# The mean of a layer norm is subtracted on VectorE, up to three tiles ahead of the multiplication, instead of on GpSimd

## The chip, the core and the metric

The kernel runs on one core of a Trainium2 chip. TensorE multiplies matrices, VectorE and ScalarE work element by element, GpSimd is a slower general engine that also issues some of the DMAs, and SyncE issues the weight loads. In the profile they are PE, DVE, ACT, POOL and SP. The metric is the device time of one execution in microseconds (us).

## The reference

One step of a two-layer decoder for 528 prompt tokens (16 of them learned meta tokens) and 32 tokens of eight running sequences, 560 columns in all, with a model width of 1024. What matters here is the layer norm. There are five of them: one on the embedded input, and two in each layer, one behind the token mixer and one behind the convolutional feed-forward block (the FFN).

```python
def layer_norm(x, g, b):
    xf = x.astype(jnp.float32)
    mu = jnp.mean(xf, -1, keepdims=True)
    var = jnp.mean(jnp.square(xf - mu), -1, keepdims=True)
    return ((xf - mu) * lax.rsqrt(var + LN_EPS) * g + b).astype(x.dtype)
...
x = layer_norm(embedded, emb_ln_g, emb_ln_b)
for l in range(DEPTH):
    mix, ... = token_mixer(x, ...)        # x @ w_in, HGRN2 heads, retention heads, @ w_o
    x = layer_norm(ALPHA * x + mix, ln1_g[l], ln1_b[l])
    ffn, ... = conv_ffn(x, ...)           # x @ w_a, x @ w_b, convolution, gelu, @ w_down
    x = layer_norm(ALPHA * x + ffn, ln2_g[l], ln2_b[l])
```

## The kernel before

Activations are stored with features on the partitions: `X` holds 8 tiles (`KT`) of 128 features by 560 columns in fp32. For the matmuls every tile is split into two fp16 parts, `XH` and the remainder `XL`, and the weights likewise into `WH` (made by ScalarE, `split_hi`, L825) and `WL` (made by VectorE, `split_lo`, L1149). TensorE forms three products for each pair of parts.

The order of the work is written out by hand. Each engine has its own program, a queue in strict order, and the engines meet through semaphores: `wait_ge(sem, n)` stops a queue until the counter is n. In the layer loop n is computed from a register, in the last norm it is a constant. `dve.drain()` makes the next VectorE instruction wait until the ones before it have written their results; it stands wherever one VectorE instruction reads what a near predecessor on the same engine wrote.

A norm, `norm_apply` on three engines and `norm_stats` on TensorE, goes like this:

- TensorE forms the mean of x (L486; for the first norm L477) and the mean of x squared (L491) over the 1024 features as matmuls with a matrix of 1/1024.
- ScalarE copies the mean to `MU` (L837) and squares it into `MSQ` (L838). VectorE subtracts `MSQ` from the mean square (L1180, two halves) and clips the variance at 0 (L1184, the "max" below). ScalarE takes its logarithm (L841) and the exponential of minus half of that (L843): `RSTD` is ready.
- GpSimd, in `norm_centre`, subtracts `MU` from the 8 tiles of `X` in place (L404). It waits for the copy of the mean alone.
- VectorE runs a loop over m: it waits for GpSimd's subtraction of tile m and multiplies the tile by `RSTD` (L1189). From m = 2 on it then waits until ScalarE is through with tile m-2 and forms `XL` of that tile (L1192).
- ScalarE applies gain and bias twice for each tile, to `XH` in fp16 (L848) and to `X` in fp32 (L849). In the last norm there is no `XH` and no `XL`.

Behind a norm, TensorE starts a `gemm_pair`: two output tiles at once, 12 matmuls for each k of the 8 tiles, in the order in which `XL` comes (`x_ready`). The matmuls are at L506. ScalarE, when it is done with the norm's tiles, goes on with the next `split_hi` (L825; behind the second norm of a layer comes first the load of the gelu table, L1079), VectorE follows with `split_lo` (L1149), and TensorE needs that `WL` for its third output tile. In a mixer VectorE's next step is `hg_gate` (L1198), behind that same `split_lo`. Behind the last norm TensorE transposes `X` (L797) once all eight tiles are done, and the result is copied and stored.

GpSimd's queue holds, in order: in each layer the first `norm_centre`, the load of the convolution state, the heads' states (a load, two products, two stores for each head, `head_states`, DMA issues at L398), the second `norm_centre`, the stores of the convolution state; and at the end the `norm_centre` of the last norm.

Of the kernel before, what the change touches and what calls it, by code (L numbers as in the profile page):

```python
# [25 lines left out]
ALU = mybir.AluOpType  # L26
ACT = mybir.ActivationFunctionType
# [3 lines left out]
DEPTH = 2  # L31
# [14 lines left out]
T = TP + TS  # L46
HALF = T // 2
KT = D_MODEL // P
# [28 lines left out]
O_TILE, F_TILE, D_TILE = 32, 40, 40 + 2 * FT  # L77

SCR_START = (11, 6, 5)
SCR_LN = (2, 1, 1)  # L80
# [90 lines left out]
def hybrid_decoder_step(nc, x_prompt, x_sample, state_hgrn, state_ret, state_conv, meta_tokens, emb_ln_g, emb_ln_b,  # L171
# [23 lines left out]
    with ExitStack() as ctx:  # L195
# [3 lines left out]
        def sem(name):  # L199
            return ctx.enter_context(nc.semaphore(name))  # L200

        tab = sb("tab", [P, n_const])
        X = sb("X", [P, KT, T])
# [29 lines left out]
        S1, S2, SQT, MU, MSQ, VAR, RSTD = B, Q, E, T1, T2, T3, QS  # L233
# [46 lines left out]
        y_ready, sq_ready, sq_used, sums_ready = sem("y_ready"), sem("sq_ready"), sem("sq_used"), sem("sums_ready")  # L280
        mu_ready, msq_ready, var_ready, rstd_ready = sem("mu_ready"), sem("msq_ready"), sem("var_ready"), sem("rstd_ready")
        ln_mul, ln_sub, ln_out, x_ready = sem("ln_mul"), sem("ln_sub"), sem("ln_out"), sem("x_ready")
        f_ready, lnf_parts, f2_ready, k_ready = sem("f_ready"), sem("lnf_parts"), sem("f2_ready"), sem("k_ready")
# [16 lines left out]
        def halves(ap):  # L300
            return ap.rearrange("p (a n) -> p a n", a=2)
# [86 lines left out]
        def _(pool):  # L388
# [10 lines left out]

            def norm_centre(n):  # L400

                pool.wait_ge(mu_ready, n + 1)
                for m in range(KT):
                    nc.gpsimd.tensor_tensor(X[:, m, :], X[:, m, :], MU[:, 0:T], ALU.subtract).then_inc(ln_sub, 1)  # L404

            def head_states(l, p, kind, s0_v, sn_v, fin_v, fin_src):
# [16 lines left out]
            with pool.Fori(0, DEPTH) as l:  # L423
                norm_centre(2 * l)

                move((acc_full, 1 + l * TILES), CIN, cin_v[ds(l * 2 * DEC_BATCH, 2 * DEC_BATCH), :], cin_in)
                with pool.Fori(0, HEADS) as p:
                    head_states(l, p, 0, s0_hg_v, sn_hg_v, fin_hg_v, SC[:, (NC - 1) * P:NC * P])
                with pool.Fori(0, HEADS) as p:
                    head_states(l, p, 1, s0_rt_v, sn_rt_v, fin_rt_v, RSB[:, :])  # L430
                norm_centre(2 * l + 1)
                move((cso_ready, l + 1), cp_v[ds(l * 2, 2), :], CSO[0:2, :], cso_stored)
                move((cso_ready, l + 1), cs_v[ds(l * 2 * DEC_BATCH, 2 * DEC_BATCH), :], CSO[2:18, :], cso_stored)
            norm_centre(2 * DEPTH)
            pool.wait_ge(fin_stored, 16 + 16 * DEPTH * 2 * HEADS)
# [366 lines left out]
        def _(act):  # L802
# [31 lines left out]
            def norm_apply(n, ot, last=False):  # L834
                act.wait_ge(ot_full, ot + 1)
                src = OT[:, :, 0:HALF]
                f(halves(MU[:, 0:T]), src, ACT.Copy).then_inc(mu_ready, 1)  # L837
                f(halves(MSQ[:, 0:T]), src, ACT.Square).then_inc(ot_read, 1)  # L838
# [305 lines left out]
        def _(dve):  # L1144
# [29 lines left out]
            def norm_apply(n, scr, last=False):  # L1174
# [8 lines left out]

                ts(VAR[:, 0:T], VAR[:, 0:T], 0.0, None, ALU.max).then_inc(var_ready, 1)  # L1184
                dve.wait_ge(rstd_ready, n + 1)
                for m in range(KT + 2):
                    if m < KT:
                        dve.wait_ge(ln_sub, n * KT + m + 1)
                        tt(X[:, m, :], X[:, m, :], RSTD[:, 0:T], ALU.mult).then_inc(ln_mul, 1)  # L1189
                    if m >= 2 and not last:  # L1190
                        dve.wait_ge(ln_out, n * KT + m - 1)
                        tt(XL[:, m - 2, :], X[:, m - 2, :], XH[:, m - 2, :], ALU.subtract).then_inc(x_ready, 1)  # L1192
# [452 lines left out]
```

## Time and profile before

| | |
|---|---|
| median of 3 runs | 1770.37 us (1768.78 to 1770.78) |
| span of the profiled execution, first to last instruction | 1765.4 us |
| the profiled execution's own time | given by its span alone; the median of the runs is 5.0 us more than that span |
| busy: TensorE | 1585.4 us, 90% of the span |
| busy: VectorE | 930.3 us, 53% |
| busy: ScalarE | 657.9 us, 37% |
| busy: GpSimd | 154.2 us, 9% |
| GpSimd's subtractions (L404) | 40 instructions, 65.2 us |
| VectorE's multiplications by `RSTD` (L1189) | 40 instructions, 727 to 1906 ns each |

A norm is a stretch of 15 to 25 us in which TensorE has nearly nothing to do. Five of them lie in the span; their first multiplications start at 40.97, 488.43, 898.59, 1338.08 and 1740.30 us. Below they are called norms 0 to 4. Norms 0 and 2 stand ahead of a token mixer, norms 1 and 3 ahead of an FFN, norm 4 ahead of the output.

In a row of the timeline the first number is the start in us, the second the duration of the piece in us. Then come engine, line, operation, what is written from what, the shapes and the count (xN). In brackets stands how long the engine had been idle before, and who ended that.

### The profile page before, as it was taken

The numbers are of one execution on the slowest core, as the hardware profiler recorded it, in microseconds if no ns is written. First come the engines' busy times: TensorE is split into PE (matmuls) and PEld (weight loads), VectorE is DVE, ScalarE is ACT, GpSimd is POOL, SyncE is SP. The second block draws the span as 40 slices with busy tenths as digits, with TensorE's granted clock in tenths as the row PEclk, the third lists the DMA queues.
The fourth block names the chain that finished last, engine by engine and source line by source line (L and its number), as shares of the span: only waits on it lengthen the run. The fifth ranks groups of instructions, "written<-read, shape, count | busy, mean of one in ns | idle before, by whom it ended". The sixth has DMA issues, their size and how long they took to land.

```text
span 1765.4 us, 31743 instructions
## 1 busy us (share of the span) xinstructions
PE 1585.4 (90%) x12187; PEld 1263.6 (72%) x12187; DVE 930.3 (53%) x1493; ACT 657.9 (37%) x936; POOL 154.2 (9%) x126
## 2 busy tenths in 40 slices
PE   4699999998879999999957999999896999999994
PEld 3577777776658888878745777777674888887883
DVE  5766744443575555533266767444366555553334
ACT  3635423232263433422154544233235443333223
POOL 3111110000020000000030111100002000000002
PEclk8789889998989999999978989999987999999997
DMA  5121231220312233223321222222121323322321
GB/s 185 51 62 51 73 109 62 84 73 26 96 50 94 95 95 95 73 79 90 97 66 48 73 73 73 76 85 73 50 74 47 96 95 95 95 80 71 98 65 51
DMA packets 175036, 137.86 MB, mean 78 GB/s; under 512 B 5064, under 2 KB 169192, under 8 KB 174776
## 3 DMA queue, kind: packets, MB, share of 16 engines
q1 hardware_dynamic: 168192, 113.46, 21.1%
q0 software_dynamic: 5408, 18.60, 3.1%
q10 hardware_dynamic: 1372, 4.95, 0.8%
q8 instruction: 41, 0.67, 0.2%
q14 instruction: 23, 0.19, 0.0%
HBM read 124.91 MB, written 12.07 MB: 78 GB/s over the span
## 4 chain that ended last, share of the span: by engine, by line
PE 76%; DVE 10%; ACT 6%; issue 4%; DVEq 3%; ACTq 1%; DMA 1%; SPq 0%
PE ACC L506 60%; PE SCR L619 2%; PE SCR L536 2%; PE OT L627 2%; ACT WH L825 1%; PE SCR L657 1%; DVE X L1189 1%; PE OT L679 1%; DVE Z L1220 1%; PE OT L595 1%; DVE Fb L1202 1%; DVE WL L1149 1%; DVEq L1259 1%; PE SCR L722 1%; PE OT L594 1%
## 5 line engine op out<-in xcount | busy, mean ns | idle before, releaser
L506 PE MATMUL ACC<-XH,WH 128*128 128x280 f16 x2432 | 503.7, 290 | 74.7 <-DVE XL L1192 43.1
L506 PE MATMUL ACC<-XL,WH 128*128 128x280 f16 x2432 | 502.6, 289 | 0.0
L506 PE MATMUL ACC<-XH,WL 128*128 128x280 f16 x2432 | 502.2, 289 | 0.0
L506 PEld LDWEIGHTS ACC<-XH,WH 128*128 128x128 f16 x2432 | 237.4, 101 | 158.7 <-DVE XL L1192 45.9
L1149 DVE SCALAR_TENSOR_TENSOR WL<-stage,WH 128x2048 f16<-128x2048 f32 (+1 forms) x116 | 245.9, 2120 | 180.8 <-ACT WH L825 169.1
L506 PEld LDWEIGHTS ACC<-XL,WH 128*128 128x128 f16 x2432 | 243.4, 100 | 58.8
L506 PEld LDWEIGHTS ACC<-XH,WL 128*128 128x128 f16 x2432 | 243.5, 100 | 58.4
L825 ACT ACTIVATE WH<-stage 128x2048 f16<-128x2048 f32 (+1 forms) x116 | 204.8, 1765 | 103.0 <-PE ACC L506 85.7
L506 PE MATMUL ACC<-shared,WH 128*128 128x280 f16 x1408 | 225.4, 283 | 0.2
L506 PEld LDWEIGHTS ACC<-shared,WH 128*128 128x128 f16 x1408 | 137.6, 98 | 30.7 <-issue 0.8
L506 PE MATMUL ACC<-shared,WL 128*128 128x280 f16 x704 | 141.3, 283 | 0.0
L404 POOL TENSOR_TENSOR X<-X,T 128x560 f32<-128x560 f32 x40 | 65.2, 1664 | 424.7 <-ACT T L837 424.7
L832 ACT ACTIVATE E<-X 128x560 f32 (+1 forms) x32 | 21.5, 671 | 192.9 <-DVEq L1171 192.9
L506 PE MATMUL ACC<-OHL,WH 128*128 128x280 f16 x512 | 87.8, 297 | 6.0 <-DVE X L1169 6.0
L1169 DVE SCALAR_TENSOR_TENSOR X<-ACC,X 128x560 f32 (+1 forms) x32 | 23.7, 740 | 109.7 <-PE ACC L506 109.0
L506 PEld LDWEIGHTS ACC<-shared,WL 128*128 128x128 f16 x704 | 68.9, 98 | 15.1
L1089 ACT ACTIVATE T<-ACC 128x560 f32<-128x560 f32 x44 | 28.1, 639 | 135.5 <-PE ACC L506 135.2
L506 PEld LDWEIGHTS ACC<-OHL,WH 128*128 128x128 f16 x512 | 51.6, 103 | 22.6 <-DVE X L1169 7.0
L1568 DVE SCALAR_TENSOR_TENSOR Fb<-ACC,Fb 128x560 f32<-128x560 f32 x22 | 16.3, 742 | 92.3 <-PE ACC L506 92.3
L413 POOL TENSOR_TENSOR VX<-KVTS,tab 32x1024 f32<-32x1024 f32 x16 | 30.2, 1886 | 306.3 <-ACTq L916 218.7
L619 PE MATMUL SCR<-VX,KVTS 32*128 32x512 f32 x64 | 39.6, 724 | 19.2 <-DVE shared L1350 19.2
L1551 DVE COPY AS<-T 128x32 f32<-128x32 f32 x44 | 8.0, 182 | 90.0 <-ACTq L1092 89.6
(241 smaller groups left out, 1870.7 us busy)
## 6 DMA issues: line engine op xcount, KB each, us to landing
stage<-in_w_in_dram SPq DMA_DIRECT2D x64, 512.0 KB, 4.8
stage<-in_w_a_dram SPq DMA_DIRECT2D x44, 512.0 KB, 4.2
stage<-in_w_b_dram SPq DMA_DIRECT2D x44, 512.0 KB, 4.6
stage<-in_w_down_dram SPq DMA_DIRECT2D x32, 384.0 KB, 3.1
stage<-in_w_down_dram SPq DMA_DIRECT2D x32, 320.0 KB, 3.4
out_dram<-shared POOLq DMA_DIRECT2D x16, 512.0 KB, 3.4
stage<-in_w_o_dram SPq DMA_DIRECT2D x16, 512.0 KB, 3.9
shared<-in_state_hgrn_dram POOLq DMA_DIRECT2D x8, 512.0 KB, 5.8
```

Source lines behind the costliest of these rows:

```text
L404: nc.gpsimd.tensor_tensor(X[:, m, :], X[:, m, :], MU[:, 0:T], ALU.subtract).then_inc(ln_sub, 1)
L413: nc.gpsimd.tensor_tensor(VX[:, :, :], KVTS[:, 1:2, :].to_broadcast([TS, DEC_BATCH, P]), bcast(seqm[0:TS, :], P), ALU.mult).then_inc(vx_re ...
L506: last = mm(ACC[:, acc, h, 0:HALF], lhs, x[:, xk + k, h * HALF:(h + 1) * HALF], start=begin, stop=end)
L536: last = mm(SCR[0:w, bank, o:o + w], keys[:, t:t + w], queries[:, t:t + w], start=True, stop=True)
L594: mm(o, SC[:, (c - 1) * P:c * P], QD[:, t:t + w], start=True, stop=False)
L619: mm(SCR[:, bank, :], KVTS[:, 0, :], VX[:, 4 * n:4 * n + 4, :].rearrange("p b v -> p (b v)"), start=True, stop=True).then_inc(scr_full, 1)
L627: last = mm(OT[:, 1, TP - SPLIT + DEC_SEQ * b:TP - SPLIT + DEC_SEQ * (b + 1)], S0b[:, b, :], qs[:, TP + DEC_SEQ * b:TP + DEC_SEQ * (b + 1) ...
L825: f(WH[:, s, 0:width], stage[:, s, 0:width], ACT.Copy, scale=W_SCALE).then_inc(w_hi[s], 1)
L832: f(SQT[:, 0:T], src, ACT.Square).then_inc(sq_ready, 1)
L1089: f(halves(AX[c][:, 2:2 + T]), ACC[:, c, :, 0:HALF], ACT.Copy, scale=INV_W)
L1149: stt(out=WL[:, s, 0:width], in0=stage[:, s, 0:width], scalar=W_SCALE, in1=WH[:, s, 0:width], op0=ALU.mult, op1=ALU.subtract).then_inc(w_l ...
L1169: stt(out=halves(row(m)), in0=ACC[:, c, :, 0:HALF], scalar=INV_W / ALPHA, in1=halves(row(m)), op0=ALU.mult, op1=ALU.add).then_inc(acc_read ...
```

## The change

GpSimd's `norm_centre` goes, with its three calls and the two semaphores `mu_ready` and `ln_sub`. VectorE does the same 40 subtractions of [128 x 560] in place. Three of them (`AHEAD`) stand between the max and the wait for `RSTD`, with one drain behind them. In the loop the subtraction of tile m+3 stands right behind the multiplication of tile m, for m = 0 to 4, each followed by a drain. Nothing else is changed; GpSimd's other work stays in its order.

```diff
+AHEAD = 3
...
-            def norm_centre(n):
-
-                pool.wait_ge(mu_ready, n + 1)
-                for m in range(KT):
-                    nc.gpsimd.tensor_tensor(X[:, m, :], X[:, m, :], MU[:, 0:T], ALU.subtract).then_inc(ln_sub, 1)
-
...
             with pool.Fori(0, DEPTH) as l:
-                norm_centre(2 * l)
-
                 move((acc_full, 1 + l * TILES), CIN, cin_v[ds(l * 2 * DEC_BATCH, 2 * DEC_BATCH), :], cin_in)
...
-                norm_centre(2 * l + 1)
                 move((cso_ready, l + 1), cp_v[ds(l * 2, 2), :], CSO[0:2, :], cso_stored)
...
-            norm_centre(2 * DEPTH)
...
             def norm_apply(n, ot, last=False):
                 act.wait_ge(ot_full, ot + 1)
                 src = OT[:, :, 0:HALF]
-                f(halves(MU[:, 0:T]), src, ACT.Copy).then_inc(mu_ready, 1)
+                f(halves(MU[:, 0:T]), src, ACT.Copy)
...
                 ts(VAR[:, 0:T], VAR[:, 0:T], 0.0, None, ALU.max).then_inc(var_ready, 1)
+                for m in range(AHEAD):
+                    tt(X[:, m, :], X[:, m, :], MU[:, 0:T], ALU.subtract)
+                dve.drain()
                 dve.wait_ge(rstd_ready, n + 1)
                 for m in range(KT + 2):
                     if m < KT:
-                        dve.wait_ge(ln_sub, n * KT + m + 1)
                         tt(X[:, m, :], X[:, m, :], RSTD[:, 0:T], ALU.mult).then_inc(ln_mul, 1)
+                    if m + AHEAD < KT:
+                        tt(X[:, m + AHEAD, :], X[:, m + AHEAD, :], MU[:, 0:T], ALU.subtract)
+                        dve.drain()
                     if m >= 2 and not last:
                         dve.wait_ge(ln_out, n * KT + m - 1)
                         tt(XL[:, m - 2, :], X[:, m - 2, :], XH[:, m - 2, :], ALU.subtract).then_inc(x_ready, 1)
```

## Rows read from the trace of the kernel before

**Rows 1.** The page: its head, and the chain that ended last, by engine.

```profile
span 1765.4 us, 31743 instructions
...
PE 76%; DVE 10%; ACT 6%; issue 4%; DVEq 3%; ACTq 1%; DMA 1%; SPq 0%
```

**Rows 2.** Windows, max to first multiplication: length, PE, PEld, DVE, ACT, POOL, clock, DMA.

```profile
37.93:40.97 3.04, 0.00 (x0) 0.00 (x0) 1.27 (x2) 1.43 (x2) 3.04 (x3) 0.50 0.83 251
485.15:488.43 3.28, 0.00 (x0) 0.00 (x0) 1.49 (x2) 1.43 (x2) 3.28 (x3) 0.72 0.00 0
895.52:898.59 3.07, 0.00 (x0) 0.00 (x0) 1.29 (x1) 1.43 (x2) 3.07 (x3) 0.50 0.15 45
1334.99:1338.08 3.09, 0.00 (x0) 0.00 (x0) 1.30 (x2) 1.43 (x2) 3.09 (x3) 0.50 0.00 0
1737.15:1740.30 3.15, 0.00 (x0) 0.00 (x0) 1.58 (x2) 1.43 (x2) 3.15 (x3) 0.83 0.00 0
```

**Rows 3.** Timeline of norm 1: GpSimd, and VectorE where GpSimd ends.

```profile
483.65 12.82 POOL L404 TENSOR_TENSOR X<-X,T 128x560 f32<-128x560 f32 x8 [64.27 <-ACT T L837]
...
495.17 1.91 DVE L1189 TENSOR_TENSOR X<-X,QS 128x560 f32<-128x560 f32 x1
497.00 0.73 DVE L1192 TENSOR_TENSOR XL<-X,XH 128x560 f16<-128x560 f32 x1
497.65 0.73 DVE L1189 TENSOR_TENSOR X<-X,QS 128x560 f32<-128x560 f32 x1
```

**Rows 4.** Window from the first multiplication to TensorE's first matmul, L1189 alone.

```profile
488.43:495.31 6.88, 5.13 (x4) 0.50 0.00 0
```

**Rows 5.** ScalarE's timeline: tile 3 of norm 1; first instruction behind norms 0 to 2.

```profile
56.09 1.89 ACT L825 ACTIVATE WH<-stage 128x2048 f16<-128x2048 f32 x1
...
497.24 0.85 ACT L848 ACTIVATE XH<-X,par 128x560 f16<-128x560 f32 x1 [2.05 <-DVE X L1189]
...
504.82 1.28 ACT L1079 ACT_TABLE_LOAD   x1
...
914.89 1.90 ACT L825 ACTIVATE WH<-stage 128x2048 f16<-128x2048 f32 x1
```

**Rows 6.** Timelines: what continues behind norms 0, 1 and 2, and its releaser.

```profile
61.33 0.74 DVE L1198 TENSOR_SCALAR Fb<-ACC 128x560 f32<-128x560 f32 x1 [1.02 <-PE ACC L506]
...
510.48 0.41 PE L506 MATMUL ACC<-XH,WH 128*128 128x280 f16 x2 [1.18 <-DVE WL L1149]
...
919.02 0.73 DVE L1198 TENSOR_SCALAR Fb<-ACC 128x560 f32<-128x560 f32 x1
```

**Rows 7.** Timeline of norm 4: all eight multiplications, and TensorE's next matmul.

```profile
1740.30 10.82 DVE L1189 TENSOR_TENSOR X<-X,QS 128x560 f32<-128x560 f32 x8 [1.57 <-ACT QS L843]
...
1752.34 5.31 PE L797 MATMUL SCR<-tab,X 128*128 128x128 f32 x24 [16.42 <-ACT X L849]
```

**Rows 8.** VectorE's timeline: a drain between two instructions; a drain and a wait.

```profile
512.89 0.18 DVE L1551 COPY AS<-T 128x32 f32<-128x32 f32 x1 [0.20 <-issue]
...
922.60 0.73 DVE L1203 TENSOR_TENSOR T<-T 128x560 f32<-128x560 f32 x1
923.41 0.45 DVE L1205 TENSOR_SCALAR T<-T 128x560 f32<-128x560 f32 x1
```

**Rows 9.** TensorE's windows in norm 1's pair: busy us (matmuls), clock, DMA.

```profile
495.31:500.30 4.99, 4.99 (x22) 0.51 0.00 0
...
500.30:509.30 9.00, 9.00 (x76) 1.00 0.00 0
```

**Rows 10.** Timelines in norm 0: a DMA that GpSimd issues, VectorE beside it.

```profile
47.69 0.93 POOL L398 DMA_DIRECT2D shared<-in_state_hgrn_dram  x1
...
47.73 0.73 DVE L1189 TENSOR_TENSOR X<-X,QS 128x560 f32<-128x560 f32 x1
```

**Rows 11.** TensorE's timeline: the matmuls of the mean, norms 1 and 3.

```profile
481.69 1.21 PE L486 MATMUL OT<-B,tab 128*128 128x280 f32 x4 [3.03 <-DVEq L1175]
...
1330.31 2.23 PE L486 MATMUL OT<-B,tab 128*128 128x280 f32 x4 [3.02 <-DVEq L1175]
```

More of the change, by code:

```diff
@@ L280, in hybrid_decoder_step @@
         y_ready, sq_ready, sq_used, sums_ready = sem("y_ready"), sem("sq_ready"), sem("sq_used"), sem("sums_ready")
-        mu_ready, msq_ready, var_ready, rstd_ready = sem("mu_ready"), sem("msq_ready"), sem("var_ready"), sem("rstd_ready")
-        ln_mul, ln_sub, ln_out, x_ready = sem("ln_mul"), sem("ln_sub"), sem("ln_out"), sem("x_ready")
+        msq_ready, var_ready, rstd_ready = sem("msq_ready"), sem("var_ready"), sem("rstd_ready")
+        ln_mul, ln_out, x_ready = sem("ln_mul"), sem("ln_out"), sem("x_ready")
         f_ready, lnf_parts, f2_ready, k_ready = sem("f_ready"), sem("lnf_parts"), sem("f2_ready"), sem("k_ready")
```

## The prediction

> **What bounds the kernel now.** I read the page first. The chain that ended last is 76% TensorE and 10% VectorE [rows 1]; GpSimd does not appear in it. So the subtractions that the change takes from GpSimd are on no path by themselves. The next view was the timeline around the five norms, engine by engine, because there TensorE waits for the other engines.
>
> In norm 1 GpSimd is busy from 483.65 to 496.47 us, 1.60 us for a tile, and VectorE's first multiplication starts at 488.43, when about three tiles are done. GpSimd stays ahead, so the multiplications do not wait for it. They run slowly instead: the one at 495.17 takes 1.91 us and its successor starts 1.83 us later; from 497.00, half a microsecond after GpSimd's end, an instruction of the same size takes 0.73 us and the next starts 0.65 us later [rows 3]. The max shows the same: 1.27 to 1.58 us in the five norms, in which GpSimd is busy throughout [rows 2], against 0.45 us for the same operation on the same shape where GpSimd is idle [rows 8]. What GpSimd costs here is the speed of VectorE beside it.
>
> The third reading is what VectorE's delay holds up. TensorE starts its pair on the first `XL`, 6.88 us behind the first multiplication (four such stretches, 6.88 to 6.89) [rows 4]. Behind the pair the releasers differ: norm 0 goes on at the end of the pair, norm 1 at `WL`, norm 2 right behind `WL` with no idle time [rows 6]. `WL` follows ScalarE's last tile, whose successor on ScalarE starts 15.12, 16.39 and 16.30 us behind the first multiplication in norms 0, 1 and 2 [rows 5], and in norm 3 as in norm 1. In norm 4 everything waits for ScalarE's last tile, 12.04 us behind the first multiplication [rows 7].
>
> **The change part by part.** *The stretch from the max to the first multiplication.* It takes 3.04, 3.28, 3.07, 3.09 and 3.15 us in norms 0 to 4 [rows 2]. After the change the max should take 0.45 us, as without GpSimd [rows 8]. An instruction of 0.73 us lets an independent successor start 0.08 before its end [rows 3]; so the first subtraction starts at 0.37 and the third ends 0.65 + 0.65 + 0.73 = 2.03 later, at 2.40. `RSTD` needs 1.77 us behind the max (3.04 - 1.27) and would be there at 2.22, so the subtractions now end last, by 0.2 to 0.4 us. A drain costs 0.08 us from end to start between two plain instructions, and 0.20 where a wait on a computed count follows [rows 8]. I take 0.20 in norms 0 to 3, where the count comes from a register, and 0.08 in norm 4, where it is constant: 2.60 and 2.48 us. Gains: 0.44, 0.68, 0.47, 0.49 and 0.67.
>
> *The loop, norms 0 to 3*, from the start of the first multiplication. A multiplication with its subtraction and a drain takes 0.65 + 0.73 + 0.08 = 1.46. Three of these rounds reach 4.38; the third drain has a wait behind it, so the first `XL` starts at 4.50 and ends at 5.23. TensorE starts 0.05 later, at 5.28 against 6.88: a gain of 1.60. Multiplication 3 starts at 5.15; rounds 3 and 4 take 0.65 + 0.73 + 0.20 + 0.65 = 2.23 each, so multiplication 5 starts at 9.61; rounds 5 and 6 take 1.30 each, and multiplication 7 runs from 12.21 to 12.94. ScalarE starts a tile 0.16 behind its multiplication (495.17 + 1.91 to 497.24 [rows 3, 5]) and takes 1.50 for it (five tiles from 497.24 to 504.82 [rows 5]). Its next instruction can start at 14.60: gains 0.52, 1.79, 1.70 and 1.79 in norms 0 to 3.
>
> *What follows.* Norm 0 continues at the pair's end: 0.44 + 1.60 = 2.04. Norms 1 to 3 hang on ScalarE's end: 0.68 + 1.79 = 2.47, 0.47 + 1.70 = 2.17, 0.49 + 1.79 = 2.28. Their pairs end 2.28, 2.07 and 2.09 earlier, and TensorE had 1.18 us of idle time in norm 1 [rows 6], so the pair does not take over.
>
> *Does the later supply starve TensorE?* A tile of the pair is 12 matmuls: 12 x 4.99 / 22 = 2.7 us at the 1.2 GHz level, with which each pair begins, and 12 x 9.00 / 76 = 1.4 at 2.4 GHz [rows 9]. `XL` comes every 2.23 us at first and then every 1.30. Tile 1 is wanted at 5.28 + 2.7 = 8.0 and there at 7.5, tile 2 is wanted near 10.4 and there at 9.7, tile 3 near 11.8 against 11.0. It holds, with half a microsecond to spare.
>
> *Norm 4.* No `XL`: five rounds of 1.46, then 0.65 each; multiplication 7 runs from 8.60 to 9.33. ScalarE does three tiles from 8.19 (0.16 behind multiplication 5), 0.75 apart (half a tile's 1.50), and ends its last, of 0.85, at 10.54; TensorE starts at 10.59 against 12.04: 1.45, with the front 2.12.
>
> *GpSimd's queue.* The subtractions stood ahead of a state load, which is issued in 0.93 us [rows 10]. It moves to the front of the norm in norms 0 and 2. The chain has 1% of DMA [rows 1], so I count an earlier arrival as nothing. At worst the issue holds VectorE for its 0.93 us in both, 1.9 in all; the multiplication at 47.73 took 0.73 beside such an issue [rows 10], so I take nothing. ScalarE's copy loses only a signal.
>
> *Sum:* 2.04 + 2.47 + 2.17 + 2.28 + 2.12 = 11.1 us. The profiled span is 1765.4 us and the median 5.0 above it; a saving inside the span passes to both: 1754.3 and **1759.2**.
>
> *Bounds.* If every drain costs 0.08, norm 0 gains 0.24 and norms 1 to 3 gain 0.48 each more: 12.8. If every drain costs 0.20, the pair starts 0.24 later, ScalarE's end comes 0.24 later, and norm 4 loses 0.7: 9.4. TensorE's clock moves it further: the four matmuls of the mean take 1.21 us in norm 1 and 2.23 in norm 3, after 3.03 and 3.02 us of idle time [rows 11], so the level there is a matter of phase. From their start to the max it is 3.46 and 4.68 us [rows 2, 11], a swing of 1.2. Norms 1 and 4 could fall to the lower level, norm 3 could rise. That makes 7.0 to 14.0.
>
> **A rule against it.** The rows say that a VectorE instruction starts 0.08 us before its independent predecessor has ended [rows 3]. The Trainium skill, "VectorE: DVE Perf Modes", section "The DRAIN you can't avoid", says that the next instruction does not start until the pipe has emptied. The trace does not agree: 0.65 us from start to start for 0.73 us of length [rows 3]. By the rule the new instructions would cost their whole length and the gain would be 6.3 us (rival 1), by the rows it is 11.1.
>
> **The rivals.**
>
> 1. *No overlap between VectorE's instructions.* Each step without a drain costs 0.73 instead of 0.65. Up to the first `XL` that is six steps (0.48 us, norm 0), up to ScalarE's end fifteen (1.20, norms 1 to 3), in norm 4 ten (0.80): 4.9 us less, 1764.1. Against it stands the spacing in [rows 3]. Chance 0.05.
> 2. *The clock does not move with the pair.* If TensorE's rise to 2.4 GHz stays at its old instant, the time gained ahead of it is run at half speed. The pairs then gain half (1.0, 1.1, 1.0, 1.0) and become what ends last; with norm 4's 2.1 the gain is 6.3 and the time 1764.1. For it: the low stretch lasts 4.99 us in norm 1, and nothing in a row ties its end to the start. Against: all four pairs begin low, wherever they lie. Chance 0.07.
> 3. *The mixers give it back.* Behind norms 0 and 2 come the mixers, where three engines hand work to each other; if a weight load or a state sets the pace there, only norms 1, 3 and 4 count: 6.9 us, 1763.5. Against it: the chain shows 1% DMA [rows 1]. Chance 0.05.
> 4. *Slower: VectorE's slowness is not GpSimd's doing* but comes from working on `X` beside ScalarE. Then the subtractions cost 1.83 a step as the multiplications do. In norm 1 ten steps and 1.1 us lead to TensorE's start, against 3.28 + 6.88 now, so it turns at 0.90 us a step; at 1.83 and a max of 1.49 it costs 10 us a norm, in norm 4 sixteen: 56 in all, 1826. For it: slow and fast instructions both occur in one norm. Against: from 497.00 VectorE is fast while ScalarE still has five tiles to do [rows 3, 5]. Chance 0.03.
> 5. *Two of the first three at once*: 1.5 us or so are left, 1769. Chance 0.05.
>
> The forecast has 0.75.
>
> **How the numbers follow.** 0.2% (3.5 us) is about what a measurement of this kernel can tell from no change. Forecast and rivals 1 to 3 are faster by more: 0.92. Rival 5 is within it: 0.05. Rival 4 is slower: 0.03. The bounds of the sum give 1756.4 to 1763.4; the range takes in rivals 1 to 3 at 1764 and a microsecond below, 1755.5 to 1764.5.
>
> **What would show it.** In the profile after: the max near 0.45 us and the first multiplication 2.5 to 2.6 behind the max's start; multiplications, subtractions and `XL` all at 0.73; TensorE's first matmul about 5.3 behind the first multiplication and never waiting for a later `XL`; ScalarE's next instruction at 14.6; stretches behind the norms unchanged in length. Multiplications near 1.8 would overthrow the reading of GpSimd; waits of TensorE inside a pair, or pairs that grow as their start moves forward, would cut the gain to about half.

## The result, and the profile after

Median 1751.57 us (1749.42 to 1752.87, 4 runs) against 1770.19 us (1768.78 to 1770.78, 4 runs) before: ratio 0.9899 [0.9883, 0.9915], 18.6 us faster. I had forecast 11.1 and a range of 1755.5 to 1764.5, so the time lies 4 us outside it on the fast side. A second measurement (e5 below) gave 0.9923 [0.9902, 0.9943], 13.9 us, inside the range. Two executions far outside all others (2114 us of e2, 6357 us of the kernel before, timed beside e1 to e4) are left out everywhere.

The page of the changed kernel, head and chain, against [rows 1]:

```profile
span 1749.8 us, 31782 instructions
...
PE 74%; DVE 10%; ACT 6%; DVEq 4%; issue 3%; ACTq 1%; DMA 1%; SPq 0%
```

The spans differ by 15.6 us. The rest of the 18.6 is that the profiled execution of before was one of its faster ones: its span was 4.8 us below the median of the four, where the changed kernel's own time, 1751.54, is 1.7 above its span.

**The norms.** Windows of the changed kernel from the max to the first multiplication, norms 0 to 4, columns as in [rows 2]:

```profile
38.45:40.93 2.48, 0.00 (x0) 0.00 (x0) 2.41 (x4) 1.43 (x2) 0.00 (x0) 0.50 1.00 302
476.11:478.59 2.48, 0.00 (x0) 0.00 (x0) 2.41 (x4) 1.43 (x2) 0.00 (x0) 0.50 0.00 0
885.68:888.17 2.49, 0.00 (x0) 0.00 (x0) 2.40 (x4) 1.43 (x2) 0.00 (x0) 0.50 0.88 274
1322.83:1325.31 2.48, 0.00 (x0) 0.00 (x0) 2.40 (x5) 1.43 (x2) 0.00 (x0) 0.50 0.00 0
1723.95:1726.43 2.48, 0.00 (x0) 0.00 (x0) 2.40 (x4) 1.43 (x2) 0.00 (x0) 1.00 0.00 0
```

All five are 2.48 or 2.49 (forecast 2.60, and 2.48 in norm 4). VectorE's timeline in norm 1, against [rows 3]:

```profile
476.11 0.45 DVE L1175 TENSOR_SCALAR T<-T 128x560 f32<-128x560 f32 x1
476.48 2.04 DVE L1177 TENSOR_TENSOR X<-X,T 128x560 f32<-128x560 f32 x3
478.59 0.74 DVE L1182 TENSOR_TENSOR X<-X,QS 128x560 f32<-128x560 f32 x1
479.25 0.73 DVE L1184 TENSOR_TENSOR X<-X,T 128x560 f32<-128x560 f32 x1
480.06 0.74 DVE L1182 TENSOR_TENSOR X<-X,QS 128x560 f32<-128x560 f32 x1
...
483.09 0.74 DVE L1188 TENSOR_TENSOR XL<-X,XH 128x560 f16<-128x560 f32 x1 [0.17 <-issue]
```

The max is at 0.45 us, the three subtractions take 2.04 (forecast 2.03), a round takes 480.06 - 478.59 = 1.47 (1.46), the first `XL` starts 4.50 us behind the first multiplication (4.50). What used to take up to 1.91 us beside GpSimd takes 0.74. TensorE and ScalarE in the same norm, against [rows 4] and [rows 5]:

```profile
471.44 2.23 PE L477 MATMUL OT<-B,tab 128*128 128x280 f32 x4 [3.03 <-DVEq L1166]
...
483.89 0.65 PE L497 MATMUL ACC<-XH,WH 128*128 128x280 f16 x2 [8.36 <-DVE XL L1188]
...
487.98 0.40 PE L497 MATMUL ACC<-XH,WH 128*128 128x280 f16 x2
```

```profile
489.04 0.85 ACT L839 ACTIVATE XH<-X,par 128x560 f16<-128x560 f32 x1 [0.59 <-DVE X L1182]
...
493.65 1.28 ACT L1070 ACT_TABLE_LOAD   x1
```

TensorE starts 483.89 - 478.59 = 5.30 us behind the first multiplication (forecast 5.28, before 6.88), ScalarE's next instruction 15.06 behind it (14.60; before 16.39). The end of norm 4, against [rows 7]:

```profile
1733.77 2.04 DVE L1182 TENSOR_TENSOR X<-X,QS 128x560 f32<-128x560 f32 x3
...
1736.95 5.24 PE L788 MATMUL SCR<-tab,X 128*128 128x128 f32 x24 [13.59 <-ACT X L840]
```

From the first multiplication to TensorE it is 10.52 us (forecast 10.59, before 12.04). Counted from the start of the max to what continues, the norms went from 9.93 to 7.77 (norm 0, the pair's start), 19.67 to 17.54, 19.37 to 17.40, 19.49 to 17.53 (ScalarE's next instruction) and 15.19 to 13.00 (TensorE): 2.16 + 2.13 + 1.97 + 1.96 + 2.19 = 10.4 us. In norm 0 a part of this does not arrive. VectorE's timeline there, against the first of [rows 6]:

```profile
57.79 2.29 DVE L1140 SCALAR_TENSOR_TENSOR WL<-stage,WH 128x2048 f16<-128x2048 f32 x1 [1.06 <-ACT WH L816]
60.00 0.73 DVE L1194 TENSOR_SCALAR Fb<-ACC 128x560 f32<-128x560 f32 x1
```

Before, the read of `ACC` waited 1.02 us for the end of TensorE's pair. Now it stands right behind `WL` with no idle time: from the max it comes 60.00 - 38.45 = 21.55 us later, before 61.33 - 37.93 = 23.40, so norm 0 is worth 1.85 and not 2.16. That makes 10.1 us for the change's own work, 1.0 less than forecast. Repeated profiles agree: with norm 0 counted to ScalarE's first read of `Fb`, the five windows sum to 97.9 us before, and to 87.8 in the change and in e4, e5, e14 and e15 below, which leave the norms as they are in the change.

**The mixers.** TensorE's windows over the two mixers, before and then after: length, busy time (matmuls), granted clock, DMA. The first window runs from ScalarE's first read of `Fb` behind norm 0 to its copy of the mean in norm 1, the second from the fourth `Z` instruction of the first head (L884, L875 after) to the copy of the mean in norm 3.

```profile
62.10:482.90 420.80, 383.57 (x2737) 0.89 0.22 70
930.90:1332.60 401.70, 361.58 (x2646) 0.92 0.23 71
```

```profile
60.80:473.70 412.90, 372.78 (x2737) 0.93 0.23 72
919.10:1320.40 401.30, 361.15 (x2646) 0.93 0.23 71
```

The change touches nothing in these windows. Yet the first is 7.9 us shorter: the same 2737 matmuls take 10.8 us less at a granted clock of 0.93 in place of 0.89. Of the 15.6 us between the spans, 8.3 lie in the mixers and 7.3 in the rest. The rest keeps 7.3 of its own 10.1: 1.3 are lost at the start of layer 2 (below), 0.5 ahead of the first max (37.93 to 38.45; kernels that still subtract on GpSimd in norm 0 reach 38.9 there), and 1.0 in the second FFN and between the copies of the mean and the max. The trace of before could have warned me: 383.57 / 2737 = 140 ns a matmul in its first mixer and 361.58 / 2646 = 137 in its second, the same code at 0.89 and 0.92.

**The start of layer 2.** ScalarE's timeline there, before and then after:

```profile
882.27 0.67 ACT L832 ACTIVATE E<-X 128x560 f32<-128x560 f32 x1 [13.79 <-DVEq L1171]
885.12 1.28 ACT L1050 ACT_TABLE_LOAD   x1 [2.18 <-issue]
```

```profile
871.10 0.67 ACT L823 ACTIVATE E<-X 128x560 f32<-128x560 f32 x1 [13.79 <-DVEq L1162]
875.29 1.28 ACT L1041 ACT_TABLE_LOAD   x1 [3.52 <-issue]
```

GpSimd's timeline of the changed kernel at that instant:

```profile
870.88 0.49 POOL L399 DMA_DIRECT2D shared<-in_state_conv_dram  x1 [124.34 <-PE ACC L497]
```

The table load comes 4.19 instead of 2.85 us behind the square: a loss of 1.34 that I had not counted. The convolution state, whose load before was issued behind norm 2's subtractions, is now loaded just there. The DMA queues between the square and the table load, before and then after:

```profile
q14 instruction: 2, 0.02, 1.4%
```

```profile
q0 software_dynamic: 32, 0.18, 16.0%
q14 instruction: 2, 0.02, 1.6%
```

Before, the first of the two 8 KB packets of the instruction queue (q14) starts 1.28 us behind the square and takes 0.31. After, the load's packets (q0) run from 0.97 to 2.07 us behind the square, and that first packet starts at 1.96 and takes 0.75.

### The profile page after: what moved, and what is told of

The parts are those of the page before. It is cut to its first block, busy times and chain, and to the rows that moved or that the text cites. A ratio compares the mean times of both kernels' runs of the same rounds, so it can differ in the third digit from the quotient of the medians.

```text
span 1749.8 us, 31782 instructions
## 1 busy us (share of the span) xinstructions
PE 1575.6 (90%) x12187; PEld 1257.8 (72%) x12187; DVE 928.3 (53%) x1533; ACT 658.4 (38%) x936; POOL 89.3 (5%) x86
## 4 chain that ended last, share of the span: by engine, by line
PE 74%; DVE 10%; ACT 6%; DVEq 4%; issue 3%; ACTq 1%; DMA 1%; SPq 0%
PE ACC L497 58%; PE SCR L527 2%; PE SCR L610 2%; PE OT L618 2%; ACT WH L816 2%; PE SCR L648 1%; PE OT L670 1%; DVEq L1255 1%; DVE Z L1216 1%; DVE X L1182 1%; DVEq L1185 1%; DVE WL L1140 1%; PE OT L586 1%; DVE Fb L1198 1%; PE SCR L713 1%
## 5 line engine op out<-in xcount | busy, mean ns | idle before, releaser
L816 ACT ACTIVATE WH<-stage 128x2048 f16<-128x2048 f32 (+1 forms) x116 | 204.9, 1766 | 103.0 <-PE ACC L497 85.7
L497 PE MATMUL ACC<-OHL,WL 128*128 128x280 f16 x256 | 54.9, 298 | 0.0
L1090 ACT ACTIVATE shared<-Fb 128x560 f32 x22 | 14.8, 671 | 94.2 <-DVEq L1566 94.2
```

The costliest lines, as they stand in the source:

```text
L497: last = mm(ACC[:, acc, h, 0:HALF], lhs, x[:, xk + k, h * HALF:(h + 1) * HALF], start=begin, stop=end)
L816: f(WH[:, s, 0:width], stage[:, s, 0:width], ACT.Copy, scale=W_SCALE).then_inc(w_hi[s], 1)
```

## The experiments

The theories: *own gain* (VectorE was slow beside GpSimd; norms alone, some 10 us), and for the rest either *the clock* (the mixers' length goes with TensorE's granted clock, which small shifts upstream can tip) or *the early loads* (GpSimd's state loads now come ahead of norms 0 and 2 and help the mixers). The expectations call the first the port theory and the last the load theory. This table has the lengths, in us, of each profiled execution, in the order of the "distance" from the end of the first window above to the start of the second. Rest is the span without the two mixers. Each row is one execution, and not always a typical one: in e4 and e8 it was the slowest of the runs, in e5 and e14 the fastest. The medians are from the first measurement and five sessions on four chips; the kernel before had 1769.1 to 1770.2 in them.

| kernel | first mixer | distance | second mixer | rest | median of runs |
|---|---|---|---|---|---|
| e16 | 415.3 | 443.1 | 406.9 | 932.0 | 1757.0 |
| e8 | 420.5 | 443.2 | 410.1 | 932.1 | 1758.8 |
| e4 | 420.6 | 443.6 | 409.7 | 934.1 | 1761.1 |
| e15 | 418.0 | 443.6 | 409.8 | 933.3 | 1760.9 |
| e12 | 423.6 | 444.6 | 401.7 | 933.5 | 1758.6 |
| e5 (the change) | 412.4 | 444.8 | 401.6 | 933.7 | 1755.9 |
| e18 | 415.4 | 444.9 | 401.5 | 935.5 | 1752.6 |
| e14 | 412.3 | 445.3 | 401.2 | 934.5 | 1756.2 |
| the change | 412.9 | 445.4 | 401.3 | 935.6 | 1751.6 |
| e2 | 423.6 | 445.6 | 404.3 | 937.9 | 1765.7 |
| e3 | 415.4 | 447.1 | 409.8 | 940.4 | 1767.2 |
| e7 | 418.2 | 447.2 | 409.6 | 938.7 | 1768.0 |
| e1 | 420.7 | 447.9 | 401.7 | 940.7 | 1766.6 |
| before | 420.8 | 448.0 | 401.7 | 942.9 | 1770.2 |
| e9 | 420.5 | 448.5 | 401.2 | 943.6 | 1767.6 |
| e17 | 423.6 | 449.2 | 404.1 | 945.6 | 1772.0 |
| e13 | 423.6 | 449.3 | 404.0 | 944.3 | 1770.9 |
| e11 | 420.4 | 451.4 | 401.7 | 946.6 | 1769.7 |
| e10 | 421.1 | 451.5 | 401.6 | 950.7 | 1773.4 |
| e6 | 412.5 | 461.4 | 409.3 | 974.2 | 1797.7 |

### e1, e2, e3: the change in some norms only

In the other norms GpSimd subtracts as before; for e1:

```diff
-norm_apply(2 * l, Scratch(base(l)))                 # VectorE subtracts
+norm_apply(2 * l, Scratch(base(l)), centred=2 * l)  # GpSimd subtracts, norms 0, 2
-norm_apply(2 * l + 1, scr_ln1(l))
+norm_apply(2 * l + 1, scr_ln1(l), centred=2 * l + 1)  # norms 1, 3
```

> VectorE subtracts in norm 4 alone, GpSimd still does norms 0 to 3, so nothing ahead of norm 4 moves. Port theory (GpSimd beside VectorE slows VectorE, and each norm has a gain of its own of about 2 us): 2.2 us less than before, near 1768, and all of it between the max and the transposes. Rival (the extra gain is spread over the whole program, for instance because GpSimd's subtractions delay something else): also near 2, so this run gives only the size of one norm's own gain.

> VectorE subtracts in norms 1 and 3 alone. Own gains 2.1 + 2.1 = 4.2 us, near 1766. Clock theory (what came on top of the norms' own 10 us is TensorE staying at 2.4 GHz for longer in a mixer, because the mixer starts at another moment): the first mixer is not moved and stays as slow as before; the second mixer is moved by 2 us and may gain or lose up to 5 us by its clock. Load theory (what came on top is due to the state loads, which GpSimd issues earlier in norms 0 and 2): 4.2 and nothing else, because norms 0 and 2 are as before.

> VectorE subtracts in norms 0 and 2 alone. Own gains 1.9 + 2.0 = 3.9 us. Clock theory and load theory both expect the extra 8 us of the first mixer here, because norm 0 is as in the full change: 1770 - 3.9 - 8 = 1758. If only 1766 is reached, the extra does not hang on norm 0.

Measured: 0.9977 [0.9966, 0.9987], 0.9964 [0.9949, 0.9978] and 0.9986 [0.9974, 0.9998], that is 4.1, 6.4 and 2.5 us, 13.0 together. In the windows of the norms that they change they gain 2.2, 4.1 and 3.8 us, together the 10.1 of the change: the parts add up where the change acts. In the rest of the span they gain 2.2, 5.0 and 2.5, against 2.1, 4.8 and 4.2 in the forecast; the loss at the start of layer 2 belongs to e3, whose loads are early. The mixers, though, moved both ways: against before, the first is 5.4 us shorter and the second 8.1 longer in e3, and both are longer in e2, by 2.8 and 2.6, though no edit stands ahead of its first mixer. Three of e2's runs took 1757.2 to 1757.7 us, eight 1765.0 to 1768.1: one kernel, two groups.

### e4, e5: the early loads, and the change again

e4 is the change with one line more; e5 is the change itself.

```diff
 with pool.Fori(0, DEPTH) as l:
+    pool.wait_ge(ln_out, (2 * l + 1) * KT)   # behind ScalarE's last tile of the norm
     move((acc_full, 1 + l * TILES), CIN, ...)
```

> The full change, but GpSimd waits for the end of norms 0 and 2 before it issues the loads of the convolution state and of the first head's state, as it did before when it subtracted first. Load theory: the first mixer gives back its 8 us, 1760. Clock theory: the first mixer keeps its gain, since its start is the same to 0.1 us. In the full change ScalarE's first instruction of the second layer came 1.3 us late while a load of the convolution state ran; if that load was the cause, this run is 1.3 us faster, 1750.3.

> The full change once more. Aligning ScalarE's instructions in the traces so far shows each mixer in one of two forms, about 8.5 us apart: in the run of before the first mixer was long and the second short, in the run of the change both short, with the loads held both long. Clock theory: which form a mixer takes hangs on where TensorE's clock happens to fall, so more runs of the full change will not all be near 1751 but show groups some 8 us apart (1750, 1758, 1767). Load theory: the early state loads make the mixers short, and all runs lie at 1749 to 1753.

Measured: e4 0.9942 [0.9927, 0.9956] (1756.19 to 1766.12), e5 0.9923 [0.9902, 0.9943] (1749.59 to 1761.17). Early loads do not make the mixers short in every run: e5's six spread over 11.6 us. The loss at the start of layer 2 is gone in e4, and still it is the slower by its median; in its profile both mixers are long.

### e6: GpSimd works beside VectorE again

The full change; in each norm GpSimd also does eight subtractions of constant tables into a tile that nobody reads.

```diff
+for m in range(KT):
+    nc.gpsimd.tensor_tensor(other[:, :], cosT, sinT, ALU.subtract)
+    pool.drain()
```

> The full change, and beside it GpSimd does eight subtractions of two constant tables into a tile of its own where it used to subtract the mean; nothing waits for them. Port theory: VectorE's max, subtractions and multiplications take 1.3 to 1.9 us each as long as GpSimd is at it, the first multiplication comes 5 to 7 us behind the start of the max instead of 2.5, and a norm is 5 to 9 us longer than in the full change. Rival (VectorE was slow because it works on the same X as ScalarE or GpSimd): VectorE stays at 0.73 and 0.45, since nothing touches X.

Measured in a single run: 1797.71 us. The rest of the span is 38.6 us longer than in the change. VectorE's timeline of e6 in norm 1, then GpSimd's:

```profile
488.99 1.74 DVE L1196 TENSOR_TENSOR X<-X,QS 128x560 f32<-128x560 f32 x1
490.66 1.90 DVE L1198 TENSOR_TENSOR X<-X,T 128x560 f32<-128x560 f32 x1
492.63 1.75 DVE L1196 TENSOR_TENSOR X<-X,QS 128x560 f32<-128x560 f32 x1
494.30 1.90 DVE L1198 TENSOR_TENSOR X<-X,T 128x560 f32<-128x560 f32 x1
496.27 0.74 DVE L1196 TENSOR_TENSOR X<-X,QS 128x560 f32<-128x560 f32 x1
```

```profile
483.26 12.34 POOL L408 TENSOR_TENSOR other<-tab 128x560 f32<-128x560 f32 x7 [0.58 <-issue]
```

VectorE is at 1.74 to 1.90 us until GpSimd ends (495.60), and at 0.74 from the next instruction on, with ScalarE working on `X` on both sides of that instant. GpSimd touches none of VectorE's data here, so it is its being at work that slows VectorE, and the prediction's rival 4 is out. VectorE's instructions start 1.67 and 1.97 us apart, 1.82 on average, and GpSimd takes 12.34 / 7 = 1.76 for one of its own: about one each in turn. The Trainium skill, "SBUF — State Buffer", section "Who interferes with whom", says that a VectorE operation with two SBUF inputs contends with a GpSimd operation that reads SBUF; these rows agree.

### e7, e11: the change, with waiting added in norms 1 and 3

Three clears in e7, six in e11, reckoned at 0.62 us each with the drain:

```diff
+for _ in range(late):                 # 3 in e7, 6 in e11; norms 1 and 3 alone
+    nc.vector.memset(S1[:, 0:T], 0.0)
+    dve.drain()
 for m in range(AHEAD):
     tt(X[:, m, :], X[:, m, :], MU[:, 0:T], ALU.subtract)
```

> The full change with three idle clears of a free tile and their drains (0.6 us each, 1.8 together) on VectorE ahead of the subtractions of norms 1 and 3. By the sum of the waits alone the time rises by 3.6 us. Clock theory: the second mixer starts 1.8 us later against the first than in the full change, so the two no longer take their forms in the same way; groups of runs 8 us apart, some runs 8 us or more above 1755. Load theory: all near 1755.

> The full change with six idle clears (measured 0.62 us each with its drain) ahead of the subtractions in the two FFN norms, 3.7 us a norm, where three cost 12 us in place of 3.7. Clock theory: twice the wait isn't twice the loss: the time can be below that of three clears, 1758 to 1766, and the mixers' heads still come only at 43.8 or 48.5 us. Rival (the three clears cost something at their place, such as the table load behind them): it lies above 1768, near 1755.9 + 2 x 12 = 1780, and the mixers are as in the kernel with three.

Measured: e7 0.9989 [0.9976, 1.0001] (1761.9 to 1770.46, 12 runs), e11 1.0011 [0.9990, 1.0031] (1761.97 to 1778.43, 12 runs). The clears are longer than reckoned, 0.75 us from start to start. The first two of e7 in norm 1:

```profile
482.07 0.53 DVE L1177 MEMSET B<- 128x560 f32 x1
482.82 0.53 DVE L1177 MEMSET B<- 128x560 f32 x1 [0.22 <-issue]
```

So norms 1 and 3 are 2.2 us longer each in e7 and 4.5 in e11; e7 waits 4.5 us in all and e11 9.0, not 3.7 and 7.4. By the medians the first 4.5 cost 12 us and the next 4.5 cost 2 (by the ratios, against e5's 0.9923, 12 and 4). Added to e5's ratio the waits alone would give 0.9948 for e7, below its interval: waiting does not simply add up. But e11's median is above the 1766 that I gave the clock theory, so that expectation missed; it lies above the rival's 1768 too, and far from its 1780. In e11's profile the second mixer is short as the clock theory allows; its rest is 11.0 us longer than the change's, 9.0 of it the waiting, and the first mixer is long.

### e8, e12: `XL` of tile m-2 ahead of the subtraction of tile m+3

```diff
 tt(X[:, m, :], X[:, m, :], RSTD[:, 0:T], ALU.mult).then_inc(ln_mul, 1)
-if m + AHEAD < KT: (subtract tile m + AHEAD, drain)
 if m >= 2 and not last: (wait, XL of tile m - 2)
+if m + AHEAD < KT: (subtract tile m + AHEAD, drain)
```

e8 has the loads held as in e4, e12 has not.

> The full change with XL of tile m-2 ahead of the subtraction of tile m+3 in VectorE's loop, and with GpSimd's state loads held until the norm is over. The first XL then starts 3.57 us behind the first multiplication instead of 4.50: norm 0 gains 0.9. Norms 1 to 3 end with ScalarE's last tile, which gains 0.4 each. The late instruction of ScalarE at the start of the second layer gains 1.3. Together 3.4 us of the stretches around the norms, by the trace; the median can differ by some us more either way with the mixers' forms.

> The full change with the low half of tile m-2 ahead of the subtraction of tile m+3 on VectorE, and the loads not held. Own gain by that order in norms 0 to 3: with the loads held the four were 9.23 us against 7.87 of the change, so 1.4 us less than the change. Clock theory: the mixers keep the change's spread of forms, so 1748 to 1760 with a median within 5 us of 1754.5. Rival (the order moves nothing): the change's own median in the repeat, 1755.9, and no own gain in the trace.

Measured: e8 0.9938 [0.9922, 0.9955], e12 0.9921 [0.9893, 0.9948] (1748.99 to 1762.27, 7 runs). In the five windows of the norms the order saves 0.9 us (87.8 to 86.9, in e8, e12 and e16 alike), less than the 1.4 that I expected of e12. In e12's norm 0 the pair starts 0.9 us earlier behind the max than in the change, but `Fb` only 0.24, since it stands behind `WL`. The rest of the span is 2.1 us shorter in e12 than in the change, but so it is by 1.9 in e5, the same kernel. In the time the order does not show: e12's first mixer came at 423.6, among the longest, and the median is not below the change's.

### e9, e10, e17: the kernel before, with waiting added in norms 1 and 3

One, three and two more copies of the mean on ScalarE, which do nothing else and were reckoned at 0.63 us each:

```diff
+for _ in range(late):                 # 1, 3, 2; norms 1 and 3 alone
+    f(halves(MU[:, 0:T]), src, ACT.Copy)
+    act.drain()
 f(halves(MU[:, 0:T]), src, ACT.Copy).then_inc(mu_ready, 1)
```

> The kernel before, in whose two FFN norms (1 and 3) ScalarE copies the mean once more (0.63 us with its drain, by the copy at 482.93 in the trace of before; nothing else is changed). Clock theory: the first mixer is untouched, and the second starts 0.6 us later against the first, which may or may not tip it: either the time stays within 1.5 us of 1771 (tipped nothing), or runs appear some 8 us away from it, at 1762 to 1764 or near 1779. Rival (waits only add up): 1770 + 2 x 0.63 = 1771.2, every run within the spread of before.

> The same with three more copies in each of the two FFN norms, 3 x 0.63 = 1.9 us a norm. Clock theory: the distance between the two mixers is 1.9 us longer than in before, as the change makes it 2 + 1 us shorter; the second mixer's form can change with nothing but waiting added: runs some 8 us below 1773.8, at 1764 to 1767 (second mixer short with the first), or some 8 us above it, near 1782. Rival (waits only add up): 1770 + 6 x 0.63 = 1773.8, with before's spread of 4 us either way.

> The kernel before with two more copies of the mean on ScalarE in norms 1 and 3: between the kernels with one (1767.6 us, distance 448.5, second mixer 401.2) and with three (1773.4, 451.5, 401.6). If the distance sets the second mixer's form: at a distance of 449.5 to 450.7 it is long, 406 to 410 us, and the time lies above both neighbours, 1775 to 1779. If the form only happened to go with it (the waits add up): between the two, 1769 to 1772, second mixer 401 to 402.

Measured: e9 0.9993 [0.9981, 1.0006], e10 1.0016 [1.0001, 1.0032], e17 1.0001 [0.9978, 1.0023]. In the profiles a copy more is 0.71 to 0.72 us (483.34 to 484.06 in e9), so the waits are 1.4, 4.3 and 2.8 us in all, and adding up would give 1.0008, 1.0024 and 1.0016. e10 and e17 agree with that, and e9's interval ends just below it: one copy costs nothing measurable, three cost 3.7 by their medians, and the second mixer is short in the profiles of e9 and e10. e17 was to put the distance between them into a long form, 406 to 410 us and 1775 to 1779. It came out at a distance of 449.2 instead of 449.5 or more, with a second mixer of 404.1 (e13, at 449.3: 404.0), and a median between its neighbours. So my number missed; the profile fits the order of the table, and the time decides nothing.

### e13 to e16, e18: which load, and the distance

e13 is the kernel before with the conv-state load alone moved ahead of the norm; e14 and e15 hold the loads of one layer in the change; e16 is e15 with the order of e8; e18 is e15 with two of e7's clears.

```diff
 # e13
+move((acc_full, 1 + l * TILES), CIN, ...)
 norm_centre(2 * l)
-move((acc_full, 1 + l * TILES), CIN, ...)
 # e14: behind the first norm; layer 2 passes at once
+pool.wait_ge(ln_out, KT)
 # e15, e16, e18: until the first tile of layer 2; layer 1 passes at once
+pool.wait_ge(acc_full, 1 + l * (TILES + 1))
```

> The kernel before, with GpSimd's conv-state load ahead of its subtractions in norms 0 and 2, and nothing else changed. If the early load makes the first mixer's short form possible (long in 7 of 7 profiles with the loads behind the norm, short in 4 of 7 with them ahead): runs some 8 us below before's 1770 appear, 1759 to 1764, with a short first mixer (412 to 415 us from its first evaluation to the next norm in place of 420 to 424). If the forms have nothing to do with the loads: before's spread, 1765 to 1773, or 1.3 us above it by the load at the start of layer 2.

> The full change with GpSimd's loads held behind norm 0 in layer 1; layer 2 is as in the change. If the early loads make the first mixer's short form possible: it is long here, and the fastest runs lie near 1757 (the kernel with the loads held in both layers: 1756.2), the median at 1758 to 1763. If not: the change's spread, 1749 to 1761, with some runs below 1752.

> The full change with the loads held in layer 2 alone, until the first tile of its projections is done. If the early loads of layer 1 make the short form of the first mixer possible: runs at the change's best, 1748 to 1750 or 1.3 us below it (the late table load of layer 2 is gone), in at least some of the runs. If not: like the kernel with the loads held in both layers, no run below 1755, median near 1761.

> The last one with the low half of tile m-2 ahead of the subtraction of tile m+3: own gains of 1.4 us more in norms 0 to 3. If layer 1's loads make the short form possible: fastest runs at 1746 to 1748, below the change's 1749.4. If not: as the same order with the loads held in both layers, 1757 to 1764.

> The change with the loads of layer 2 held (1760.9 us, distance 443.6, second mixer 409.8), and two idle clears, 1.24 us, in each of the two FFN norms. If the distance sets the form: at 444.8 the second mixer is short, 401 to 402 us, and 2.5 us more of waiting make the kernel faster, 1760.9 + 2.5 - 8.3 = 1755, with runs near 1750. If the waits add up: 1763.4, second mixer 410 us, no run below 1757.

Measured: e13 1.0010 [0.9993, 1.0026], e14 0.9933 [0.9916, 0.9951], e15 0.9951 [0.9934, 0.9968], e16 0.9935 [0.9921, 0.9948], e18 0.9906 [0.9872, 0.9941].

My idea that layer 1's early loads make the first mixer short fell: with them held (e14) it is 412.3, and the runs reach down to 1749.83. It looked as if layer 2's load mattered: with it held, the second mixer is the longer in four profiles of four (409.7, 410.1, 409.8 and 406.9 in e4, e8, e15 and e16). e13 and e15 show the 1.34 us as well: ScalarE's table load at the start of layer 2 in e13, then in e15.

```profile
885.11 0.67 ACT L831 ACTIVATE E<-X 128x560 f32<-128x560 f32 x1 [13.79 <-DVEq L1170]
889.26 1.28 ACT L1049 ACT_TABLE_LOAD   x1 [3.48 <-issue]
```

```profile
876.54 0.67 ACT L824 ACTIVATE E<-X 128x560 f32<-128x560 f32 x1 [13.79 <-DVEq L1163]
879.12 1.28 ACT L1042 ACT_TABLE_LOAD   x1 [1.91 <-issue]
```

4.15 us with the early load, in the kernel before too; 2.58 with the load held, in the changed one.

e18 decides between load and distance. Its load is held and the 1.34 us are not paid, as in e15, but its two clears (1.5 us a norm in its profile, 3.0 in all) bring the distance back to 444.9. TensorE's windows over the second mixer, e15 and then e18:

```profile
922.92:1332.70 409.78, 372.55 (x2646) 0.89 0.22 70
```

```profile
921.59:1323.06 401.47, 361.42 (x2646) 0.92 0.23 71
```

The same 2646 matmuls take 11.1 us less, at 0.92 in place of 0.89. The kernel that waits 3.0 us more has a median of 1752.57 where e15 has 1760.87, and all its runs (1749.4 to 1758.3) lie below e15's median. The two were timed in different sessions, on different chips: the kernel before stood at 1769.5 and 1769.1 in them, and the intervals of the two ratios just overlap, but five of e18's six runs are below all six of e15's (from 1756.85). So a delay of that size, without the load, does what the load seemed to do.

## Why the prediction was right, and where it failed

**Mechanism: right.** The max at 0.45, the front at 2.48, rounds of 1.47, TensorE at 5.30 against 5.28: VectorE's speed beside GpSimd was the cost, and e6 puts it back. Rival 1 is out: the second instruction of a round starts 0.66 us after a first one of 0.74 (478.59 to 479.25). The Trainium skill, "VectorE: DVE Perf Modes", section "The DRAIN you can't avoid", says that the next operation does not start until the pipe is empty, and also that one that is not held starts earlier. The prediction gave the first half alone; the 0.66 us here agree with the second. Rival 2 is out: the pair of norm 1 starts low, but is at the higher level 487.98 - 478.59 = 9.4 us behind the first multiplication, where before it took 500.30 - 488.43 = 11.9 [rows 4, 9]. Rival 3 is the opposite of what happened. With rivals 1 to 3 out, so is rival 5. Norm 4 came 2.19 us earlier, 2.12 forecast. (By its own sum the forecast is 1759.3 and not 1759.2.)

**ScalarE's end in norms 1 to 3: mis-sized by up to 0.46 us each.** I had ScalarE end 1.50 us behind multiplication 7. From tile 5 on it is ScalarE that sets its own pace: it starts tile 5 at 489.04 and needs 1.50 for each of three tiles, while VectorE goes on at 1.30. So its next instruction is at 15.06 and not at 14.60; with the front quicker by 0.12 each (2.48 for 2.60), norms 1 to 3 gain 6.1 in place of 6.9. Norm 0 turned on the same thing: "Norm 0 continues at the pair's end" no longer holds once `WL`, which follows ScalarE, ends last, and 2.04 became 1.85.

**GpSimd's queue: "I take nothing" failed, by 1.3 us.** I looked at what the earlier loads do to VectorE in the norms and not at what they meet where they now stand; the load of the convolution state, which comes first, was not in the prediction at all. It is issued 4.4 us ahead of that table load, and before 21 behind it (906.60, the end of norm 2's subtractions). The step from the square to the table load is 3.86 to 4.36 us in the eight profiles with the load there and 2.58 to 2.87 in the other twelve. The first instruction packet ends 2.4 to 2.9 us behind the square in the eight and 1.3 to 1.6 in the twelve, and in all 20 the table load starts 1.1 to 1.5 us behind that end. Whether the packet is what ScalarE waits for is not shown; no run moved it by itself.

**The step that failed: "TensorE's clock moves it further ... a swing of 1.2".** I counted the clock in the matmuls of the mean alone and expected the stretches behind the norms to stay "unchanged in length". The swing of the mean's matmuls is real: 2.23 us in norm 1 instead of 1.21. But the same clock moves the first mixer by up to 11 us and the second by up to 9, as the table shows, and each is about as much as all that I forecast; between before and the change it was 7.9 us in the first. A fair range would have been open to it on both sides.

Part of the miss is the draw. The first measurement's four executions lie at 1749.4 to 1752.9 us, with granted clocks of 0.938 to 0.942 over the whole execution. Of e5's six, the same kernel, two are at 1749.6 and 1749.8 (0.941), three at 1755.7 to 1757.4 (0.934) and one at 1761.2 (0.930).

That a wait upstream can turn the form of the second mixer is shown by e18, which turned it by waiting alone. What decides it is less sure. The 20 profiles order by the distance, long at 443, short at 445, long at 447, short at 448 and 451, long at 461, with 404 in between at 445.6 and 449.2. That order was read off them afterwards, and of the two kernels built to test it e18 came out as forecast and e17 did not. The instant at which the mixer starts orders them less well: it is short at 919.1 us (the change), 406.9 at 919.5 (e16), short at 921.6 (e18) and long at 922.9 (e15). Before and change both have a short one, so it adds 0.4 us to the gain; without the 1.34 us that the change loses at the start of layer 2 it is long (the profiles of e4 and e15).

The first mixer gives the rest. With norm 0 on GpSimd it took 420.5 to 423.6 us in all of 7 profiles, on average 422.0; with norm 0 on VectorE 412.3 to 423.6 in 13, on average 416.7. On average that is 5.3 us, which with 7.3 to 9.2 in the rest of the span (the change and e5) and 0.4 makes 13.0 to 14.9; the two measurements gave 18.6 and 13.9. **Open:** why a single run of the first mixer takes its form. Its 20 lengths fall into five groups: 412.3 to 412.9, 415.3 to 415.4, 418.0 to 418.2, 420.4 to 421.1 and 423.6 us. The change, e7 and e11 run the same code up to its end and came at 412.9, 418.2 and 420.4.

None of these kernels is shown to beat the change: the lowest ratios, 0.9906 (e18) and 0.9921 (e12), are not below its 0.9899.

## What to carry to other kernels

Before forecasting a change of a few us, compare repeated stages of the same code in one trace: if their length differs with TensorE's granted clock, as 140 against 137 ns a matmul here, put that difference into the range on both sides. An edit upstream is then worth its own work plus what it tips, and only a profile, split into the stretches that the edit touches and those it does not, tells the two apart; one median does not. When an operation leaves a queue, what stood behind it moves forward as well: look at what it meets there.

## What the runs showed of the hardware that I had not expected

- Waiting can make the kernel faster: 3.0 us of idle clears took e15's 1760.9 us to 1752.6 (e18, in another session), through a granted clock of 0.92 in place of 0.89 over a mixer of 2646 matmuls.
- VectorE beside GpSimd falls to GpSimd's pace even when the two share no data: 1.82 us from start to start, where GpSimd takes 1.76 for one of its own, against 0.66.
- A DMA issued by GpSimd at the start of layer 2 goes with a delay of some 1.3 us in ScalarE's next instruction (3.86 to 4.36 us behind its predecessor with it, 2.58 to 2.87 without, in 20 profiles). The profile names no releaser; an 8 KB packet of the instruction queue is late along with it.
